# Three output projections of a four-layer model moved to tokens on partitions with a seven-product scheme, on Trainium2

## The reference, cut to what matters

```python
# first block, layer i (0: even mixer, 1: odd mixer); only x goes on after layer 1
y = even_mixer(u, uc, ...) or odd_mixer(u, uc, ...)     # ends in concat(...) @ w_out
h = h + gt_m * rms_norm(y, g_post_mix[i])
f = swiglu(modulate(rms_norm(h, g_pre_ffn[i]), sh_f, sc_f), w_gate, w_up, w_down)
h = h + gt_f * rms_norm(f, g_post_ffn[i])

# second block, each layer
mix = concat([y_attn, y_conv, y_pool]) @ w_out[i]       # 256 x 1024 by 1024 x 1024
h = h + rmsnorm(mix, norm_mix_post[i])
m = square(relu(rmsnorm(h, norm_mlp_pre[i]) @ w_up[i])) @ w_down[i]
h = h + rmsnorm(m, norm_mlp_post[i])
h = h + sigmoid(h @ ple_gate[i]) * (p[i] @ ple_proj[i])
```

## Time and profile before

| | |
|---|---|
| median of 3 runs | 2348.47 us (2347.08 to 2350.25) |
| profiled execution, its own time | 2351.62 us |
| its span | 2349.8 us |
| busy: PE, DVE, ACT, POOL | 2224.0, 959.2, 462.2, 103.6 us |
| mean granted clock of TensorE | 0.976 of full speed |
| loads | 272.28 MB, 116 GB/s |

### The profile page before, as it was taken

The page is one execution under the profiler, slowest core; times in us unless marked ns, Lnnn a source line. Parts: engine busy times, 40 slices in busy tenths (PEclk is TensorE's granted clock), DMA queues, the critical chain, the costliest instruction groups (busy, mean ns, idle before and its releaser), DMA issues.

```text
span 2349.8 us, 33017 instructions
## 1 busy us (share of the span) xinstructions
PE 2224.0 (95%) x14328; PEld 1562.0 (66%) x14328; DVE 959.2 (41%) x1745; ACT 462.2 (20%) x987; POOL 103.6 (4%) x126
## 2 busy tenths in 40 slices
PE   6999999899899999979998999998899999889998
PEld 3447877464688884446577884686785478678646
DVE  1565445552644440032232115584324428622343
ACT  2333211451200000021252000223110022311001
POOL 0003333000300000000000000000000000000000
PEclk9999999999999999989998999999899999999999
DMA  7221444303622221113103445331345433134552
GB/s 315 72 72 56 147 146 166 133 14 132 178 78 85 90 90 72 72 54 108 54 19 108 154 150 174 122 126 54 108 146 191 151 139 126 55 103 148 179 179 72
DMA packets 39215, 272.28 MB, mean 116 GB/s; under 512 B 4768, under 2 KB 6176, under 8 KB 6944
## 3 DMA queue, kind: packets, MB, share of 16 engines
q1 hardware_dynamic: 36896, 262.16, 31.6%
q0 software_dynamic: 1312, 3.15, 0.7%
q10 hardware_dynamic: 864, 4.87, 0.5%
HBM read 268.58 MB, written 1.05 MB: 115 GB/s over the span
## 4 chain that ended last, share of the span: by engine, by line
PE 87%; DVE 8%; ACT 3%; issue 1%; DMA 1%; ACTq 0%; DVEq 0%
PE banks L399 27%; PE banks L1153 11%; PE banks L962 11%; PE banks L1059 7%; PE banks L1645 5%; PE banks L2292 4%; PE banks L1328 2%; PE banks L1352 2%; PE banks L437 2%; PE banks L611 1%; PE banks L751 1%; PE banks L1348 1%; PE banks L485 1%; DVE arena L2444 1%; PE banks L766 1%
## 5 line engine op out<-in xcount | busy, mean ns | idle before, releaser
L399 PE MATMUL banks<-normed,weight_ring 128*128 128x256 f32 (+1 forms) x1296 | 305.3, 399 | 12.9 <-DVE normed L549 11.8
L399 PEld LDWEIGHTS banks<-normed,weight_ring 128*128 128x128 f32 x1296 | 250.1, 194 | 68.4 <-issue 19.1
L399 PE MATMUL banks<-arena,weight_ring 128*128 128x512 f32 (+1 forms) x480 | 179.1, 535 | 0.8 <-DVE arena L843 0.8
L1059 PE MATMUL banks<-normed,weight_ring 128*128 128x256 f32 x704 | 154.7, 383 | 3.4 <-ACT normed L561 3.4
L1059 PEld LDWEIGHTS banks<-normed,weight_ring 128*128 128x128 f32 x704 | 135.5, 193 | 22.7 <-ACT normed L561 3.8
L2292 PE MATMUL banks<-normed,weight_ring 128*128 128x256 f32 x640 | 144.5, 386 | 5.8 <-DVE normed L549 2.9
L399 PEld LDWEIGHTS banks<-arena,weight_ring 128*128 128x128 f32 x480 | 91.1, 190 | 88.0 <-issue 83.5
L2292 PEld LDWEIGHTS banks<-normed,weight_ring 128*128 128x128 f32 x640 | 123.1, 193 | 25.0 <-issue 4.6
L962 PE MATMUL banks<-arena 128*128 128x512 f32 x280 | 131.2, 592 | 0.0
L381 DVE TENSOR_TENSOR roots<-roots,squares 128x256 f32<-128x256 f32 (+1 forms) x35 | 18.6, 532 | 264.9 <-ACT squares L387 264.9
L1645 PE MATMUL banks<-normed,weight_ring 128*128 128x512 f32 x288 | 126.1, 593 | 0.0
(11 more groups left out here) (401 smaller groups left out, 3182.1 us busy)
## 6 DMA issues: line engine op xcount, KB each, us to landing
weight_ring<-in_weights SPq DMA_DIRECT2D x249, 1024.0 KB, 4.9
constants<-in_const ACTq DMA_DIRECT2D x1, 2209.5 KB, 12.4
residual<-in_tokens ACTq DMA_DIRECT2D x1, 2048.0 KB, 12.8
mix<-in_rpb POOLq DMA_DIRECT2D x32, 64.0 KB, 9.4
out<-residual SPq DMA_DIRECT2D x1, 1024.0 KB, 4.8
branch<-arena POOLq DMA_DIRECT2D x1, 512.0 KB, 4.8
normed<-in_ple POOLq DMA_DIRECT2D x1, 512.0 KB, 3.6
vector_params<-in_vectors ACTq DMA_DIRECT2D x1, 223.0 KB, 5.8
```

The lines of the kernel that those rows point to most:

```text
L399: mm = pe.matmul(K.psum[lo:hi, banks[m % nb], 0:T], K.block(first[m] + k)[:, lo:hi], rhs(k), start=(k == 0), stop=(k == n_k - 1))
L1059: mm = pe.matmul(K.bank(i % 4, T), K.block(first[i] + k), u[:, k, 0:T], start=(k == 0), stop=(k == KT - 1))
```

## The change

The output projections of the odd mixer and of the two sparse mixers become `TokenProjection`s with n = 4 pairs. The even mixer's keeps its form. A new class `OutProjection` makes them: `ahead` is called inside the mixer just before its attention stage and puts sums on GpSimd, which wait for the attention's own inputs; `run` comes after the attention. In the sparse mixers GpSimd makes the sums of weights of pairs 0 and 1 and those of tokens of pairs 0 and 1; for this the four tiles of convolution and pooling are now first in `mix` and in the rows of the weights, and two pairs are `ahead`. In the odd mixer it makes the sums of weights of pairs 0 and 1, DVE makes all sums of tokens after the attention, in groups of three pairs and one, and three pairs are `ahead`. DVE makes the sums of weights of pairs 2 and 3. The weights of these projections are packed in rows and start on a chunk.

`scale_stage` uses the same room as four buffers of squares where a tile has 256 tokens. In every `TokenProjection` DVE now scales quarters 2, 3 and 0, and ACT quarter 1. Areas in the sparse mixer are laid out in another order, and several semaphores share names, which changes no wait.

```diff
+SPARSE_ATTENTION = 7168
@@ weight_blocks
-            out.append(pack_tiles(x["w_out_odd"][0], columns(D), rows))
+            out.append(np.zeros((-sum(len(a) for a in out) % CB, P, P), np.float32))
+            out.append(pack_rows(x["w_out_odd"][0][rows], columns(D)))
...
-        rows = np.concatenate([np.array(t) for t in paired(0)] + [np.arange(512, 1024)])
-        out.append(pack_tiles(x["w_out_2"][i], columns(D), rows))
+        rows = np.concatenate([np.arange(512, 1024)] + [np.array(t) for t in paired(0)])
+        out.append(np.zeros((-sum(len(a) for a in out) % CB, P, P), np.float32))
+        out.append(pack_rows(x["w_out_2"][i][rows], columns(D)))
@@ scale_stage
+    square = K.square if T > S else K.square.rearrange("p i (j n) -> p (i j) n", n=S)
+    n_square = square.shape[1]
...
-                if i >= K.n_square:
-                    act.wait_ge(summed.sem, su + i - K.n_square + 1)
-                act.activation(K.square[:, i % K.n_square, 0:T], src, ACT.Square).then_inc(squared.sem, 1)
+                if i >= n_square:
+                    act.wait_ge(summed.sem, su + i - n_square + 1)
+                act.activation(square[:, i % n_square, 0:T], src, ACT.Square).then_inc(squared.sem, 1)
@@ TokenProjection.add_weights, the same in add_tokens
-    def add_weights(self, dve, p):
+    def add_weights(self, dve, p, name="vector"):
...
-        step = K.in_turn(dve, "vector")
+        step = K.in_turn(dve, name)
@@ TokenProjection.run, tensor
+            scaled = {2: ("taken_out_by_vector", 1), 3: ("taken_out_by_vector", 2), 0: ("taken_out_by_vector", 3), 1: ("taken_out_by_scalar", 1)}
             for half in (1, 0):
-                done = 1 if half else 2
-                pe.wait_ge(sg["taken_out_by_vector"].sem, at["taken_out_by_vector"] + done)
                 for k in range(KT):
-                    if k == 4:
-                        pe.wait_ge(sg["taken_out_by_scalar"].sem, at["taken_out_by_scalar"] + done)
+                    if k % 4 == 0:
+                        name, count = scaled[2 * half + k // 4]
+                        pe.wait_ge(sg[name].sem, at[name] + count)
@@ scalar
-            for j, q in enumerate((3, 1)):
-                half = q // 2
-                act.wait_ge(sg["inverted"].sem, at["inverted"] + j + 1)
-                act.activation(y[:, q], y[:, q], ACT.Copy, scale=inverse[:, half:half + 1]).then_inc(sg["taken_out_by_scalar"].sem, 1)
+            act.wait_ge(sg["row_inverses"].sem, at["row_inverses"] + 2)
+            act.activation(y[:, 1], y[:, 1], ACT.Copy, scale=inverse[:, 0:1]).then_inc(sg["taken_out_by_scalar"].sem, 1)
@@ vector
-                dve.tensor_scalar(y[:, 2 * half], y[:, 2 * half], iv, None, ALU.mult).then_inc(sg["taken_out_by_vector"].sem, 1)
+                for q in (2, 3) if half else (0,):
+                    dve.tensor_scalar(y[:, q], y[:, q], iv, None, ALU.mult).then_inc(sg["taken_out_by_vector"].sem, 1)
@@ odd_mixer, and the same in sparse_mixer
+    ahead(r)
     return attention_stage(K, rounds, [R.mixed[:, i:i + 2, :] for i in (0, 2, 4, 6)], r + table_ready, buf)
@@ sparse_mixer
-    return attention_stage(K, rounds, [mix[:, 0:4, t * P:t * P + P] for t in range(2)], ready, buf)
+    return attention_stage(K, rounds, [mix[:, 4:8, t * P:t * P + P] for t in range(2)], ready, buf)
@@ program
+        class OutProjection:
+            def __init__(self, mix, groups, n_early, regions):
+                fa = Area(*regions)
+                self.weight_sums, self.token_sums = [[fa.get(512) for _ in range(4)] for _ in range(2)], [fa.get(4, P) for _ in range(3)]
+                self.mix, self.groups, self.n_early, self.last = mix, groups, n_early, []
+            def ahead(self, ready):
+                K.taken += -K.taken % CB
+                n = self.n_early
+                to = self.to = TokenProjection(K, self.mix, KT, self.token_sums, self.weight_sums, token_y, lambda k: [] if k < 2 * n else self.last,
+                                               self.groups, n)
+                def sums(pool):
+                    need(pool, ready)
+                    to.add_weights(pool, 0, "gpsimd")
+                    if n == 2:
+                        to.add_tokens(pool, 0, "gpsimd")
+                    to.add_weights(pool, 1, "gpsimd")
+                K.add(gpsimd=sums)
+            def run(self, gain, r):
+                self.last += r
+                to = self.to
+                def sums(dve):
+                    need(dve, r)
+                    dve.wait_ge(to.sg["f_weights"].sem, to.at["f_weights"] + 2)
+                    if self.n_early == 2:
+                        dve.wait_ge(to.sg["f_tokens"].sem, to.at["f_tokens"] + 1)
+                    for g in range(1 if self.n_early == 2 else 0, 2):
+                        to.add_tokens(dve, g)
+                K.add(vector=sums)
+                root_table(K)
+                return to.run(h, gain, r)
...
+                wo = OutProjection(R.mixed, [(0, 3), (3, 4)], 3, (R.u, R.y[:, 2048:]))
+                r = odd_mixer(K, R, u, r, kr, table_ready, wo.ahead)
                 R.arena = full
-                r = matmul_stage(K, KT, KT, lambda k: R.mixed[:, k, :], S, lambda e, m, ps: e.activation(y[:, m, 0:S], ps, ACT.Copy), r, squares=True)
-                r, tiles = residual(K, h, S, S, y, gain(1, 1), r)
+                r, tiles = wo.run(gain(1, 1), r)
...
+            wo = OutProjection(R.mix2, [(0, 2), (2, 4)], 2, (R.arena[:, SPARSE_ATTENTION:],))
+            r = sparse_mixer(K, R, layer, u2, r, kr, wo.ahead)
+            r, tiles = wo.run(plain("norm_mix_post"), r)
```

More of the change, by code:

```diff
@@ L484, in tensor @@
                 pe.wait_ge(squared.sem, sq + i + 1)
-                pe.matmul(K.bank(4 + g % 2, T), lhs, K.square[:, i % K.n_square, 0:T], start=(t == 0), stop=(t == len(tiles) - 1)).then_inc(summed.sem, 1)
+                pe.matmul(K.bank(4 + g % 2, T), lhs, square[:, i % n_square, 0:T], start=(t == 0), stop=(t == len(tiles) - 1)).then_inc(summed.sem, 1)
                 i += 1
@@ L655, in scalar @@
         for k in range(KT):
-            act.activation(out[:, k, :], h[:, k, :], ACT.Square).then_inc(sg["n_square"].sem, 1)
-        act.wait_ge(sg["n_sum"].sem, at["n_sum"] + 1)
-        act.activation(r, K.bank(5), ACT.Sqrt, bias=K.c("eps"), scale=1.0 / D).then_inc(sg["n_root"].sem, 1)
+            act.activation(out[:, k, :], h[:, k, :], ACT.Square).then_inc(sg["squared"].sem, 1)
+        act.wait_ge(sg["summed"].sem, at["summed"] + 1)
+        act.activation(r, K.bank(5), ACT.Sqrt, bias=K.c("eps"), scale=1.0 / D).then_inc(sg["rooted"].sem, 1)
         piece.keep(act)
@@ L2702, in program @@
             kr, _ = modulated_norm(K, h, S, S, plain("norm_mix_pre"), None, u2, [], tiles)
-            r = sparse_mixer(K, R, layer, u2, r, kr)
-            r = matmul_stage(K, KT, KT, lambda k: R.mix2[:, k, :], S, lambda e, m, ps: e.activation(y2[:, m, :], ps, ACT.Copy), r, squares=True)
-            r, tiles = residual(K, h, S, S, y2, plain("norm_mix_post"), r)
+            wo = OutProjection(R.mix2, [(0, 2), (2, 4)], 2, (R.arena[:, SPARSE_ATTENTION:],))
+            r = sparse_mixer(K, R, layer, u2, r, kr, wo.ahead)
+            r, tiles = wo.run(plain("norm_mix_post"), r)
             kr, _ = modulated_norm(K, h, S, S, plain("norm_mlp_pre"), None, u2, [], tiles)
```

50 lines of the change are left out of this document (26 added, 24 removed).

## The result

| | before | changed |
|---|---|---|
| median of 4 runs each | 2349.36 us (2347.08 to 2353.01) | 2317.88 us (2315.31 to 2327.57) |
| ratio, 95% interval | | 0.9872 (0.9841 to 0.9904) |
| profiled execution, own time | 2351.62 us | 2315.31 us |
| its span, mean granted clock | 2349.8 us, 0.976 | 2313.4 us, 0.984 |

The change makes the kernel 31.5 us faster by the medians; 2319.5 us was forecast, from a sum of 29.3 us. The two profiled executions differ by more, 36.3 us.

The account below looks back on a forecast made before the run. TensorE carries 87% of the chain of waits, so fewer matmuls or shorter stretches off TensorE pay. 13.1 + 11.4 + 2.8 + 1.2 + 0.8 = 29.3 us saved, median forecast 2319.5 us, range 2310 to 2334.

Parts of the forecast that it names:

- Fewer products: Three mixers' output projections: 56 instructions in 24.04 us against 27.91, early start; saves 4.5, 4.5 and 4.0, 13.1 us.
- rival (2): Projections: four pairs too short to hide DVE's sums of weights; 8 us lost, 2327.5 us; chance 0.08.
- Rival (4): Early products wait for the last group, 0.7 us a mixer, quarters only swap places: 3 us less, 2322.5; within forecast's 0.67.
- The wait for the last group: Before each mixer's projection: attention's last matmul to first product takes 0.10 us in place of 0.77.
- GpSimd: Sums beside the attention: 12.2 us per sparse mixer, 9.5 in the odd one, ended before the attention; cost nothing.
- Rival (3): GpSimd's additions hold up the attention: price up to 33.9 us, median 2353, slower; chance 0.03.
- Attention unchanged at about 20 us: Sign of being right: the attention keeps its length, about 20 us, beside GpSimd's sums.
- The tail: Last product to norm's root taken as 7.9 us; three mixers save 11.4 us together, FFN site 2.8.
- Rival (1): Clock stays low in the new tails: three mixers save 0.8 together, FFN site nothing; median 2332.6; chance 0.20.
- The buffers: Four buffers of squares let ACT run on; norm behind first embedding takes 3.5 us instead of 4.7, saving 1.2.
- The gate sites: Two sites where transposes end at +3.65 in place of +4.05: 0.4 us each, 0.8 us.
- may shift by 1 us a site, five sites, either way: Stages behind norms start with some microseconds at low clock; possible shift, left out of the sum.

Follow-up runs that it names:

- odd_three_buffers: Changed kernel with three buffers of weight sums in the odd mixer, GpSimd making three sets; 2322.91 us (one run).
- no_early: Changed kernel in which TensorE waits for the attention's last group before the projection's first product; 2325.73 us, 0.9892.
- gpsimd_long: Changed kernel with GpSimd making pair 1's weight sums three times and DVE's token sums not waiting for GpSimd's weights; 2325.36 us (one run).
- dve_sums: Changed kernel with GpSimd unused, DVE making all sums after the attention; 2323.32 us, 0.9880 of before.
- two_buffers: Changed kernel with two buffers of squares in place of four; 2330.67 us (one run).
- only_projections: Changed kernel with two buffers of squares and ACT scaling quarters 3 and 1 again, leaving only the three new projections; 2331.56 us, 0.9913 of before.
- only_buffers: Kernel before with four buffers of squares and nothing else; 2345.53 us, 0.9978.
- before_busy_tails: Kernel before with seven useless matmuls in each token_norm, keeping TensorE busy in the old tails; 2345.72 us (one run).
- busy_gaps: Changed kernel with six useless matmuls behind the sums of squares of the five norms over 256 tokens; 2315.20 us, 0.9849.
- warm_everywhere: Changed kernel with three odd-mixer weight-sum buffers and useless matmuls behind 256- and 512-token norms and ahead of the sparse mixers' convolutions; 2304.60 us, 0.9807.

## Why the prediction was right

**Fewer products: right.** 56 instructions in 24.04 us and the start right behind the attention: 24.24 us in the sparse layers against 24.14 in the text, 4.4 us saved against 4.5. The chain has them as one piece, so rival (2) is out for the sparse layers. In the odd mixer the stall was there, where the text put it, but 0.66 us instead of 0.5 (odd_three_buffers takes it away); saved 3.8 instead of 4.0. Rival (4) is out too: the early products start right behind the attention, and the quarters save 0.33 us a site. The term came to 12.6 us, not 13.1. The wait for the last group, priced at 0.77 - 0.10 = 0.67, cost 0.85 in no_early.

**GpSimd: right in its sum, not in its prices.** The text read 1.19 us for an addition from rows 8, but the line is a multiplication with one operand from the constants, and GpSimd's instruction in rows 9 is a multiplication too. An addition of 128x512 took 1.27 us, and one of 256 wide 0.72, not 0.66. That gives 8 x 1.27 + 4 x 0.72 = 13.0 us per sparse mixer, still 7.8 us early, hence free. Rival (3) is out: the attention's DVE reductions took 424 ns beside it and 425 without it, and gpsimd_long lost nothing with 10 us more of GpSimd's work. "Attention unchanged at about 20 us" did not hold in the profile (21.3 twice), but not for GpSimd's sake: it was 22.8 without GpSimd (dve_sums) and 19.94 with most of it (gpsimd_long), each time as the clock was. What the text left open is what GpSimd's part gives: 4.7 us (dve_sums).

**The tail: the right number from a mean that no tail showed.** The text took 7.9, between +7.45 at full clock and +8.9 with one low stretch. All tails came at +7.85 at full clock. Two errors cancelled, which is luck: the full-clock tail was underrated by 0.4 us, and the low stretch did not come. The first is in the last step: the squares start at +4.09 (text +3.97), and eight tiles take 3.74 us, not 8 x 0.44 = 3.49. The difference is a start from rest: in two_buffers' chain two instructions take 0.71 us behind a wait and 0.45 without one, and eight tiles take 3.45 at the embedding, where TensorE comes straight from other matmuls. The sum left this start out. The second error: one in three sites had fallen in the trace of before, so a fall was given weight. The old split of the scaling does fall (9 of 21 tails, gates included), the new one never did (0 of 54). The transposes' pause shrinks from 0.50 to 0.17 us; the text had worked out when quarters 3 and 0 are ready, but put the value of it at 0.4 us of waiting and not at the clock. Measured: 3.7 + 4.0 + 3.9 = 11.6 us (forecast 11.4) and 2.85 (2.8). In the FFN's 2.85 about 1.2 us are the low clock of the one old execution that was profiled (only_projections and only_buffers had it at 1.00 there).

**Rival (1), low clock in the new tails,** did not come in any profile with the new scaling, and the clock was a third of the old tail's excess, 1.0 to 1.3 of 3.7 to 4.0 us (before_busy_tails), not all of it. Against 0 of 36 tails a chance of 0.20 looks too large; the trace of before, where one site of three fell, did not tell. (Its price has a slip: with +11.4 for each tail the three mixers would save 1.0 us together, not 0.8.)

**The buffers:** 1.2 us at the embedding, as forecast (4.66 to 3.45). In the tails they are worth 1.2 too, inside the 11.6. The three buffer terms that the text folded into one tail can't be read from one another: alone in the old mixers' tails they gave 0.5 to 0.8 (only_buffers), in the new ones 1.20 (two_buffers), since there nothing else bounds the squares.

**The gate sites:** 0.33 us each, not 0.4.

**Sum:** 12.6 + 11.6 + 2.85 + 1.2 + 0.7 = 28.9 us against 29.3. The medians moved by 31.5, the profiled executions by 36.3. The rest is what the text left out of the sum, "may shift by 1 us a site, five sites, either way". It does shift, but by more and at more places: the same kernel, profiled twice, is 15.8 us apart with all changed steps equal to 0.02 us. The place is right (stage starts at 51 to 65 instructions in 14 us, that is up to 3 us each), the number of places was too small: behind the pause before the convolutions an attention of small matmuls takes between 19.9 and 22.8 us, and the even mixer's and odd mixer's stages shift too. So the 2.2 us between 31.5 and 29.3 can't be assigned to any step; the interval of the ratio is 15 us wide.

## What to carry to other kernels

Split a tail by the clock before pricing its form: give TensorE useless matmuls in the old kernel and see how much the landmark moves. A step that takes waiting out of TensorE's small work can be worth more than its length: here 0.33 us went, and with the new split of the scaling a low clock that had come in 9 of 21 tails and had cost 0.4 to 1.3 us each (that the shorter pause is the reason is not shown). Where executions of one kernel lie further apart than the change is worth, compare landmarks in the chain, not times; and fill the remaining pauses, which here gave another 14 us and made the time repeatable.

## What the runs showed of the hardware

- TensorE's pauses cost more behind them than in them. A pause of 2.9 us behind a norm (3.4 in the first block) was followed by a stage start with 51 to 59 instructions in 14 us (clock 0.78 to 0.90) in some executions and with 65 (1.00) in others; with six useless matmuls in the pause it was 65 at all five sites in both kernels that had them (busy_gaps, warm_everywhere).
- The 14 matmul instructions behind a pause of 6.8 us took 5.5 to 6.3 us at a clock of 0.51 to 0.59 in 26 of 26 places, and 3.3 us at 1.00 with the pause filled to 1.15 us (warm_everywhere). The attention of small matmuls behind them took 19.9, 21.3 or 22.8 us (clock 1.00, 0.92, 0.85; 12, 6 and 8 of the 26), differently from one execution to the next and even between the two layers of one. With the pause filled it took 19.94 and 19.93.
- A DVE addition with both operands in SBUF went from 0.42 to 1.15 and 1.37 us beside GpSimd's additions, and these from 1.27 to 1.33 us: DVE, whose additions each started behind one of GpSimd's, loses the time (gpsimd_long).
- Two matmul instructions of 256 columns took 0.45 us behind others and 0.71 us behind a wait, so each start behind a wait costs some 0.26 us (two_buffers).
- TensorE's products read SBUF while DVE waited for GpSimd, and were not slower: 24.24 us in gpsimd_long as without it.
